# A hybrid diffusion layer with experts: the branch test, the gate and the last scatter at the end of the kernel

## The chip, the cores and the metric

The kernel runs on one core of one Trainium2 chip. The metric is the time of one launch on the device, in microseconds (us). TensorE (PE in the rows, PEld for its weight loads) multiplies matrices, VectorE (DVE), ScalarE (ACT) and GpSimd (POOL) work elementwise, and SyncE (SP) issues DMA transfers. A row with a q behind the engine's name (PEldq, ACTq) is an instruction that the engine's sequencer handles by itself, such as a branch.

## The reference, cut to what matters

128 context tokens and 128 latent tokens of width 1024 go through one layer. All 256 tokens share the weights, but each of the two groups has its own modulation vectors. The change touches only the end of this:

```python
# channel mixer: top 4 of 32 experts, combine holds the weight of each expert for each token
def expert(acc, xs):
    wu, bu, wd, bd, g = xs
    ...
    y = ((up + 1.0) * glu) @ wd + bd
    return acc + g[:, None] * y, None

xp = xp + gt_f * moe(h, *moe_args)      # gt_f: one vector of 1024 for the whole group
...
xs = xs + gt_f * moe(h, *moe_args)
y_prompt = rmsnorm(xp, g_final)         # x / sqrt(mean(x*x) + eps) * g_final
y_sample = rmsnorm(xs, g_final)
```

All matrices are float32. The 32 experts' weights are 384 MB of the 460 MB that the kernel reads.

## The kernel before, in words

The kernel is written engine by engine: each engine has its own instruction stream, and the order between them is made by semaphores alone (`wait_ge`, `then_inc`). No planner moves anything.

After the mixing part comes the loop over experts. It takes them in pairs, 16 pairs, two pairs to one turn of the loop (`Fori(0, PAIRS // BODY)`, 8 turns). One pair is a pass:

- TensorE gathers up to 64 tokens for each of the two experts with one-hot matmuls (`gather`, L1335), multiplies them by the up weights (L1372), transposes, and multiplies by the down weights (L1410). The last result stands in PSUM banks 6 and 7 (`YB`).
- ScalarE copies it to `yb` (L654), 128 slots by 1024, and raises `y_ready`.
- TensorE scatters the slots back to their tokens with the weights of the router: `scatter`, L1342, four matmuls of 128x512 into banks 4 to 7 (`GB + n`), for token group t = n // 2 and column half n % 2. The scatter of a pass is done in the middle of the next pass, so the scatter of the last pass is left over for the end. VectorE adds the four banks into `acc` (L975).
- SyncE streams the weights through a ring of 16 slots of 1 MB (L329), each load waiting until its slot is free (`moe_free`).

An expert has 64 places. If more tokens than that chose one expert, further rounds of all 16 passes are needed. Each engine has the code for up to three further rounds behind its loop, nested in `If`s (`further_rounds`, the test is L280), and steps over it when the count doesn't ask for it. In the runs here no further round is taken: each matmul group of the loop appears 16 times.

At the end, with the loop and the test behind:

- VectorE multiplies `acc` by the gate `gtf` and adds it to x (L1045, L1046), without the last pass. Then `last_add(t)` takes the last scatter: for each half a multiplication by the gate (L1052), a wait for it to finish (`link`), and an addition to x (L1053).
- ScalarE squares each half of x and sums it (`squares`, L603). VectorE adds the two sums of a token group (`mean_of_halves`, L699) and GpSimd raises that to the power -1/2 (`root`, L392).
- VectorE multiplies x by the final gain (`last_gain`, L1060, two halves). The scale by the root is shared: ScalarE does the low half (L674, `fin_lo`), VectorE the high half (`last_scale`, L1065, `fin_hi`).
- SyncE stores each group when both halves are done (L342), and waits for both stores.

Of the kernel before, what the change touches and what calls it, by code (L numbers as in the profile page):

```python
# [1 line left out]

# [7 lines left out]
ALU = mybir.AluOpType  # L23
ACT = mybir.ActivationFunctionType
# [3 lines left out]
D = 1024  # L28
# [11 lines left out]
HALF = 512  # L40
# [39 lines left out]
def layer_kernel(nc, A_x_prompt, A_x_sample, A_cache_k, A_cache_v, A_c, A_c_ctx, A_w_ada, A_b_ada, A_g_mix,  # L80
# [12 lines left out]
    with ExitStack() as ctx:  # L93
# [36 lines left out]
        def in_slot(s, at, *shape):  # L130
# [6 lines left out]
            if len(shape) == 3:  # L137
# [12 lines left out]
        hid = region(8960, D)  # L150
        hT = region(9984, KB, P)
        yb = region(11008, D)

        sgA = region(0, KB, TOK)
        sgB = region(2048, KB, TOK)
# [97 lines left out]
        cur_ready, glu_ready = sem("cur_ready"), sem("glu_ready")  # L253
        fin_ss, fin_lo, fin_hi, last_scat, stored = (sem("fin_ss"), sem("fin_lo"), sem("fin_hi"), sem("last_scat"),
                                                     sem("stored"))
        xf_ready = sem("xf_ready")
        kv_stored, bias_t, bias_copied = sem("kv_stored"), sem("bias_t"), sem("bias_copied")

        GB, YB = 4, 6
# [211 lines left out]
        def _(act):  # L471
# [150 lines left out]
            nc.scalar.activation(woT[0:E, :, :], ps[0:E, 6, 0:TOK].rearrange("p (a b) -> p a b", a=2),  # L622
                                 ACT.Copy).then_inc(woT_ready, 1)
            act.wait_ge(L["bdn"], 16)
            act.sem_inc(y_ready, 1)

            def xg_out(b, H, q):

# [4 lines left out]
            def body(I, r):  # L633
                P0 = act.snap(I * BODY)
                n0 = act.snap(I * BC)
                H0 = act.snap(P0 * 2 + (r + 1))
                for h in range(BODY):
                    Pn, H = P0 + h, H0 + 2 * h
                    xg_out(1, H, h)
                    for b in range(2):  # L640
                        act.wait_ge(g_ready, Pn * 2 + (b + 1))
                        nc.scalar.activation(sig[:, b * HALF:(b + 1) * HALF], gate[:, b * HALF:(b + 1) * HALF],  # L642
                                             ACT.Sigmoid, scale=ALPHA).then_inc(sig_ready, 1)
                    xg_out(0, H + 1, (h + 1) % 2)
                    act.wait_ge(woT_done, Pn + 2)
                    nc.scalar.activation(woT, ps[:, YB, 0:TOK].rearrange("p (a b) -> p a b", a=2),
                                         ACT.Copy).then_inc(woT_ready, 1)
                    for b in range(2):
                        act.wait_ge(hT_done, Pn * 2 + (b + 1))
                        nc.scalar.activation(hT[:, 4 * b:4 * b + 4, :],  # L650
                                             ps[:, GB + b, :].rearrange("p (a b) -> p a b", a=4),
                                             ACT.Copy).then_inc(hTe_ready, 1)
                    act.wait_ge(moe_free, n0 + (RING + (h + 1) * PC))
                    nc.scalar.activation(yb.rearrange("p (a b) -> p a b", a=2), ps[:, YB:YB + 2, :],  # L654
                                         ACT.Copy).then_inc(y_ready, 1)

            xg_out(0, 0, 0)
            more = read_flags(act)
# [20 lines left out]
        def _(dve):  # L679
# [352 lines left out]
            def run(r):  # L1032

                dve.wait_ge(oh_ready, r * (PAIRS + 1))
                V.tensor_scalar(tab[:, :, 0:4], tab[:, :, 0:4], float(CAP), None, ALU.subtract).then_inc(tab_ready, 1)
                dve.wait_ge(tab_ready, r)
                dve.wait_ge(gath_done, r * (2 * PAIRS + 1))
                one_hots(0, r * (PAIRS + 1))
                with dve.Fori(0, PAIRS // BODY) as i:
                    body(i + r * (PAIRS // BODY), i, r)  # L1040
                dve.wait_ge(acc_done, 4 * (r + 1) * PAIRS)
            further_rounds(dve, more, run)


            link(V.tensor_tensor(acc, acc, gtf[:, :, :], ALU.mult))  # L1045
            link(V.tensor_tensor(x[:, :, :], x[:, :, :], acc, ALU.add))  # L1046

            def last_add(t):
                for n in range(2):
                    c = slice(n * HALF, (n + 1) * HALF)  # L1050
                    dve.wait_ge(last_scat, 2 * t + n + 1)
                    link(V.tensor_tensor(acc[:, t, c], ps[:, GB + 2 * t + n, :], gtf[:, t, c], ALU.mult))  # L1052
                    V.tensor_tensor(x[:, t, c], x[:, t, c], acc[:, t, c], ALU.add).then_inc(fin_ss, 1)  # L1053

            def last_gain(t):

# [8 lines left out]
                V.tensor_scalar(x[:, t, HALF:D], x[:, t, HALF:D], rstd[:, t:t + 1], None, ALU.mult).then_inc(fin_hi, 1)  # L1065

            dve.wait_ge(L["gfin"], 16)
            last_add(0)
            last_add(1)
            mean_of_halves(0, 1)  # L1070
            last_gain(0)
            last_scale(0)
            mean_of_halves(1, 1)
            last_gain(1)
            last_scale(1)


        @block.tensor
        def _(pe):
# [256 lines left out]
                                 oh[:, t, :], start=(t == 0), stop=(t == 1))  # L1336
                ins.then_inc(gath_done, 1)

            def scatter(done):
                for n in range(4):  # L1340
                    t = n // 2
                    mm(ps[:, GB + n, :], woT[:, t, :], yb[:, (n % 2) * HALF:(n % 2 + 1) * HALF],  # L1342
                       start=True, stop=True).then_inc(done, 1)

            def body(I, r):
                P0 = pe.snap(I * BODY)
# [8 lines left out]
                for h in range(BODY):  # L1355
                    Pn, G, H = P0 + h, G0 + h, H0 + 2 * h

                    pe.wait_ge(u_read, Pn + 1)
                    pe.wait_ge(sel_ready, Pn + 1)
                    for n in range(4):  # L1360
                        for a in range(2):
                            mm(ps[CAP * a:CAP * a + CAP, n, :], selbuf[:, a, :], bparts[:, n * HALF:(n + 1) * HALF],
                               start=True, stop=False)
                    for kk in range(KB):
                        if kk % 4 == 0:
                            pe.wait_ge(xg_ready, H + (kk // 4 + 1))
                        if kk == 3:
                            gather(G - 1, 1)
                        w = [chunk(h * PC + 2 * kk + a) for a in range(2)]
                        for n in range(4):  # L1370
                            for a in range(2):
                                ins = mm(ps[CAP * a:CAP * a + CAP, n, :], xgT[:, h, kk, CAP * a:CAP * a + CAP],  # L1372
                                         w[a][:, n * HALF:(n + 1) * HALF], start=False, stop=(kk == KB - 1))
                                if n == 3:
                                    ins.then_inc(moe_free, 1)

                    pe.wait_ge(y_ready, Pn + 1)
                    pe.wait_ge(woT_ready, Pn + 1)
                    scatter(scat_done)

                    pe.wait_ge(acc_done, Pn * 4 + 1)
                    gather(G, 0)

                    pe.wait_ge(wo_ready, Pn + 1)
                    pe.wait_ge(acc_done, Pn * 4 + 3)
                    for t in range(2):
                        ins = tp(ps[:, YB, t * P:(t + 1) * P], wo[:, t, :], ident[:, :])  # L1387
                    ins.then_inc(woT_done, 1)

                    for f in range(KB):  # L1390
                        if f % 4 == 0:
                            pe.wait_ge(hid_ready, Pn * 2 + (f // 4 + 1))
                            if f == 0:
                                pe.wait_ge(xg_ready, H + 3)
                            else:
                                pe.wait_ge(acc_done, Pn * 4 + 2)
                        ins = tp(ps[:, GB + f // 4, (f % 4) * P:(f % 4 + 1) * P], hid[:, f * P:(f + 1) * P], ident[:, :])
                        if f % 4 == 3:
                            ins.then_inc(hT_done, 1)

                    pe.wait_ge(woT_ready, Pn + 2)
                    pe.wait_ge(acc_done, Pn * 4 + 4)
                    for f in range(KB):
                        if f % 4 == 0:
                            pe.wait_ge(hTe_ready, Pn * 2 + (f // 4 + 1))
                        if f % 2 == 0:
                            w = [chunk(h * PC + UPC + f + a) for a in range(2)]
                        for n in range(2):
                            for a in range(2):
                                ins = mm(ps[CAP * a:CAP * a + CAP, YB + n, :], hT[:, f, CAP * a:CAP * a + CAP],  # L1410
                                         w[a][:, (f % 2) * D + n * HALF:(f % 2) * D + (n + 1) * HALF],
                                         start=(f == 0), stop=(f == KB - 1))
                                if f % 2 and n == 1:
                                    ins.then_inc(moe_free, 1)
# [3 lines left out]
            more = read_flags(pe)  # L1418
            with pe.Fori(0, PAIRS // BODY) as i:
                body(i, 0)  # L1420
            pe.wait_ge(y_ready, 1 + PAIRS)
            pe.wait_ge(woT_ready, 1 + PAIRS)

            def run(r):
                gather(r * (PAIRS + 1), 0)
                with pe.Fori(0, PAIRS // BODY) as i:
                    body(i + r * (PAIRS // BODY), r)
                pe.wait_ge(y_ready, 1 + (r + 1) * PAIRS)
                pe.wait_ge(woT_ready, 1 + (r + 1) * PAIRS)
            further_rounds(pe, more, run)  # L1430
            scatter(last_scat)


_INS = ['x_prompt', 'x_sample', 'cache_k', 'cache_v', 'c', 'c_ctx', 'w_ada', 'b_ada', 'g_mix', 'w_in', 'w_pool',
# [24 lines left out]
```

## Time and profile before

| | |
|---|---|
| time, median of 3 runs | 1213.35 us (1212.09 to 1216.87) |
| span of the profiled execution | 1214.1 us |
| time given for the profiled execution beside its span | none |
| PE busy | 1066.4 us (88%) |
| DVE busy | 271.5 us (22%) |
| ACT busy | 161.5 us (13%) |
| mean granted TensorE clock | 0.984 of full speed |
| moved by DMA | 460.24 MB, mean 379 GB/s |
| end of the last matmul of the expert loop | 1194.6 us |
| from there to the end of the span | 19.5 us |

A start is counted from the first instruction of the profiled execution. "Idle before" is the time for which the engine had no busy instruction ahead of the one shown, and the arrow names what released it; "issue" means that the profile shows nothing that it waited for. A float32 matmul of 128x512 shows as two records.

### The profile page before, as it was taken

The page shows a single profiled execution, that of the slowest core. Times are in us where ns is not written, and L with a number is a line of the kernel's source. Part 1 is how long each engine was busy: PE and PEld are TensorE (multiplying, and loading weights), DVE is VectorE, ACT ScalarE, POOL GpSimd, SP SyncE. Part 2 cuts the span into 40 slices and gives each one's busy share as a digit, 9 for nine tenths or more (in the row PEclk, how much of TensorE's full clock was granted, in tenths as well). Part 3 has the DMA queues.
Part 4 walks back from the last instruction along what each step waited for, and adds up shares of the span by engine and source line. Part 5 has one row for each costly group of instructions (what it writes and reads, how often), then busy time and mean ns, then how long its engine had stood idle before and what let it go on. Part 6 is the DMA issues. An engine that isn't in the chain of part 4 may idle for free.

```text
span 1214.1 us, 14268 instructions
## 1 busy us (share of the span) xinstructions
PE 1066.4 (88%) x5363; PEld 523.7 (43%) x5363; DVE 271.5 (22%) x580; ACT 161.5 (13%) x275; POOL 54.6 (4%) x81
## 2 busy tenths in 40 slices
PE   4799999999999989797979797979798989898985
PEld 1574987554443434343434343433333333333331
DVE  2132856422021120202020202020202020202024
ACT  1101433211011101101110111011101110111011
POOL 3027000000000000000000000000000000000000
PEclk8899999989999999999999999999999999999998
DMA  9998553979999999999999999999999999999991
GB/s 356 363 345 314 211 202 112 368 308 419 415 419 416 420 415 420 415 421 415 421 415 420 415 421 414 421 414 421 414 422 414 421 414 421 414 421 413 422 412 59
DMA packets 88085, 460.24 MB, mean 379 GB/s; under 512 B 7404, under 2 KB 7448, under 8 KB 52120
## 3 DMA queue, kind: packets, MB, share of 16 engines
q1 hardware_dynamic: 86392, 455.12, 92.5%
q0 software_dynamic: 1024, 3.29, 1.0%
q10 hardware_dynamic: 640, 1.44, 0.4%
q8 instruction: 17, 0.28, 0.1%
q14 instruction: 12, 0.10, 0.0%
HBM read 458.26 MB, written 1.57 MB: 379 GB/s over the span
## 4 chain that ended last, share of the span: by engine, by line
SPq 57%; PE 26%; DMA 6%; issue 6%; DVE 4%; ACT 1%; POOL 0%; POOLq 0%; DVEq 0%; ACTq 0%
SPq L329 55%; PE ps L1372 7%; PE ps L1410 5%; DMA ring<-in_w_in_dram 4%; PE ps L1120 2%; PE ps L1303 2%; DMA ring<-in_w_up_dram 2%; PE ps L1117 1%; PE ps L1135 1%; PE ps L1137 1%; PE ps L1136 1%; SPq L321 1%; PE ps L1095 1%; PE ps L1335 1%; PE ps L1266 1%
## 5 line engine op out<-in xcount | busy, mean ns | idle before, releaser
L1372 PE MATMUL ps<-ring,arena 128*64 128x512 f32 x2048 | 460.8, 595 | 73.7 <-DMA ring<-in_w_up_dram 73.7
L1372 PEld LDWEIGHTS ps<-ring,arena 128*64 128x64 f32 x2048 | 160.0, 136 | 352.9 <-issue 349.2
L1410 PE MATMUL ps<-ring,arena 128*64 128x512 f32 x1024 | 224.9, 597 | 6.7 <-ACT arena L650 6.7
L1410 PEld LDWEIGHTS ps<-ring,arena 128*64 128x64 f32 x1024 | 86.6, 138 | 134.7 <-issue 134.7
L964 DVE COPY cur<-tab 128x8 f32 (+1 forms) x17 | 2.9, 171 | 448.9 <-PE ps L1335 448.8
L1000 DVE TENSOR_SCALAR arena<-ps 128x512 f32<-128x512 f32 x32 | 20.6, 686 | 329.6 <-PE ps L1372 329.6
L1335 PEld LDWEIGHTS ps<-arena 128*128 128x128 f32 x528 | 64.1, 195 | 21.5 <-issue 19.2
L1342 PE MATMUL ps<-arena 128*128 128x512 f32 x136 | 64.5, 618 | 5.0 <-issue 5.0
L1335 PE MATMUL ps<-arena 128*128 128x128 f32 x528 | 67.4, 282 | 0.4 <-DVE arena L968 0.4
L642 ACT ACTIVATE arena<-arena 128x512 f32<-128x512 f32 x32 | 19.6, 630 | 338.3 <-DVE arena L1000 338.3
L630 ACT ACTIVATE arena<-ps 128x512 f32<-128x512 f32 x33 | 19.7, 597 | 260.3 <-PE ps L1335 260.3
L1120 PE MATMUL ps<-ring 128*128 128x256 f32 x192 | 44.0, 392 | 6.0 <-issue 6.0
L654 ACT ACTIVATE arena<-ps 128x1024 f32<-128x1024 f32 x16 | 16.4, 1024 | 221.4 <-PE ps L1410 221.4
L1342 PEld LDWEIGHTS ps<-arena 128*128 128x128 f32 x136 | 25.1, 194 | 44.2 <-issue 44.2
L455 POOL COPY selbuf<-sel 96x128 bf16 x16 | 4.7, 291 | 867.7 <-DVE arena L1002 854.7
L1120 PEld LDWEIGHTS ps<-ring 128*128 128x128 f32 x192 | 37.8, 198 | 12.2 <-issue 6.8
L975 DVE TENSOR_TENSOR arena<-ps,arena 128x512 f32<-128x512 f32 x64 | 40.9, 680 | 0.0
L1135 PE MATMUL ps<-parts 128*128 128x256 f32 x128 | 36.7, 287 | 0.6 <-DVE parts L801 0.6
L1095 PE MATMUL ps<-ring 128*32 128x512 f32 x192 | 27.1, 689 | 10.5 <-DMA ring<-in_w_ada_dram 10.5
L1136 PE MATMUL ps<-parts 128*128 128x256 f32 x128 | 36.2, 283 | 0.0
L1137 PE MATMUL ps<-parts 128*128 128x256 f32 x128 | 36.2, 283 | 0.0
L1387 PE MATMUL ps<-ident,arena 128*128 128x128 f32 x32 | 7.0, 301 | 24.9 <-DVE arena L975 24.9
(212 smaller groups left out, 746.9 us busy)
## 6 DMA issues: line engine op xcount, KB each, us to landing
ring<-in_w_up_dram SPq DMA_DIRECT2D x256, 1024.0 KB, 24.1
ring<-in_w_down_dram SPq DMA_DIRECT2D x128, 1024.0 KB, 20.5
ring<-in_w_ada_dram SPq DMA_DIRECT2D x24, 1024.0 KB, 13.9
ring<-in_w_in_dram SPq DMA_DIRECT2D x16, 1024.0 KB, 12.5
ring<-in_w_out_dram SPq DMA_DIRECT2D x4, 1024.0 KB, 6.7
ring<-in_w_pa_dram SPq DMA_DIRECT2D x2, 1024.0 KB, 7.3
ring<-in_w_pb_dram SPq DMA_DIRECT2D x2, 1024.0 KB, 6.6
out_dram<-x SPq DMA_DIRECT2D x2, 512.0 KB, 2.6
```

The lines of the kernel that those rows point to most:

```text
L329: sp.dma_start(dst, src).then_inc(moe_loaded[n % RING], 16)
L975: V.tensor_tensor(acc[:, t, c], ps[:, GB + n, :], acc[:, t, c], ALU.add).then_inc(acc_done, 1)
L1095: ins = mm(ps[32 * q:32 * q + 32, bank, :], cs[:, kk, :], w[:, q * HALF:(q + 1) * HALF], start=(kk == 0), stop=(kk == KB - 1))
L1120: ins = mm(ps[:, bank + b // 2, (b % 2) * TOK:(b % 2 + 1) * TOK], wk[:, b * P:(b + 1) * P], hTm[:, kk, :], start=(kk == 0), stop=(kk == KB ...
L1135: mm(out, w_top[:, n % 2, kk, :], hT_top[:, kk, :], start=(kk == 0), stop=False)
L1136: mm(out, w_top[:, n % 2, kk, :], hT_rest[:, kk, :], start=False, stop=False)
L1137: ins = mm(out, w_rest[:, n % 2, kk, :], hT_top[:, kk, :], start=False, stop=(kk == KB - 1))
L1303: ins = mm(ps[:, 2 * t + n, :], sgA[:, kk, t * P:(t + 1) * P], wo_[kk // 2][:, kk % 2, n * HALF:(n + 1) * HALF], start=(kk == 0), stop=(kk ...
L1335: ins = mm(ps[:, GB + b, (j % 4) * P:(j % 4 + 1) * P], h2[:, t, j * P:(j + 1) * P], oh[:, t, :], start=(t == 0), stop=(t == 1))
L1342: mm(ps[:, GB + n, :], woT[:, t, :], yb[:, (n % 2) * HALF:(n % 2 + 1) * HALF], start=True, stop=True).then_inc(done, 1)
L1372: ins = mm(ps[CAP * a:CAP * a + CAP, n, :], xgT[:, h, kk, CAP * a:CAP * a + CAP], w[a][:, n * HALF:(n + 1) * HALF], start=False, stop=(kk ...
L1410: ins = mm(ps[CAP * a:CAP * a + CAP, YB + n, :], hT[:, f, CAP * a:CAP * a + CAP], w[a][:, (f % 2) * D + n * HALF:(f % 2) * D + (n + 1) * H ...
```

## The change

Four edits, all at the end, and one small one in each pass:

1. TensorE no longer waits for the last `yb` ahead of the test for further rounds. The test comes directly behind the loop, and the waits come after it. The same wait goes into the code of the further rounds for TensorE and VectorE.
2. The copy of `yb` out of PSUM (L654) is made in two halves of 128x512, in every pass, and each half raises `y_ready`. All counts of `y_ready` are doubled.
3. The last scatter is written on its own. VectorE first multiplies `yb` by the gate of each group into a new buffer `yg` (`last_weight`, four products of 128x512; `yg` lies over `gate` and `sig`, which are free by then). TensorE scatters `yg` into banks 0 to 3 instead of 4 to 7. Behind each scatter VectorE has one addition of PSUM to x in place of a multiplication and an addition.
4. VectorE takes the mean of the second group ahead of the high-half scale of the first: the order mean, gain, scale, mean, gain, scale becomes mean, gain, mean, gain, scale, scale.

```diff
+        yg = region(6912, 2, D)
...
-            act.sem_inc(y_ready, 1)
+            act.sem_inc(y_ready, 2)
...
-                    nc.scalar.activation(yb.rearrange("p (a b) -> p a b", a=2), ps[:, YB:YB + 2, :],
-                                         ACT.Copy).then_inc(y_ready, 1)
+                    for b in range(2):
+                        nc.scalar.activation(yb[:, b * HALF:(b + 1) * HALF], ps[:, YB + b, :],
+                                             ACT.Copy).then_inc(y_ready, 1)
...
+            def last_weight(t):
+                for n in range(2):
+                    c = slice(n * HALF, (n + 1) * HALF)
+                    dve.wait_ge(y_ready, 2 * PAIRS + n + 1)
+                    V.tensor_tensor(yg[:, t, c], yb[:, c], gtf[:, t, c], ALU.mult).then_inc(yg_ready, 1)
 
             def last_add(t):
                 for n in range(2):
                     c = slice(n * HALF, (n + 1) * HALF)
                     dve.wait_ge(last_scat, 2 * t + n + 1)
-                    link(V.tensor_tensor(acc[:, t, c], ps[:, GB + 2 * t + n, :], gtf[:, t, c], ALU.mult))
-                    V.tensor_tensor(x[:, t, c], x[:, t, c], acc[:, t, c], ALU.add).then_inc(fin_ss, 1)
+                    V.tensor_tensor(x[:, t, c], x[:, t, c], ps[:, 2 * t + n, :], ALU.add).then_inc(fin_ss, 1)
...
             dve.wait_ge(L["gfin"], 16)
+            last_weight(0)
+            last_weight(1)
             last_add(0)
             last_add(1)
             mean_of_halves(0, 1)
             last_gain(0)
-            last_scale(0)
             mean_of_halves(1, 1)
             last_gain(1)
+            last_scale(0)
             last_scale(1)
...
-                    pe.wait_ge(y_ready, Pn + 1)
+                    pe.wait_ge(y_ready, Pn * 2 + 2)
                     pe.wait_ge(woT_ready, Pn + 1)
-                    scatter(scat_done)
+                    scatter()
...
             with pe.Fori(0, PAIRS // BODY) as i:
                 body(i, 0)
-            pe.wait_ge(y_ready, 1 + PAIRS)
-            pe.wait_ge(woT_ready, 1 + PAIRS)
...
             further_rounds(pe, more, run)
-            scatter(last_scat)
+            pe.wait_ge(woT_ready, 1 + PAIRS)
+            for n in range(4):
+                t, c = n // 2, slice((n % 2) * HALF, (n % 2 + 1) * HALF)
+                pe.wait_ge(yg_ready, n + 1)
+                mm(ps[:, n, :], woT[:, t, :], yg[:, t, c], start=True, stop=True).then_inc(last_scat, 1)
```

## Rows read from the trace of the kernel before

**Rows 1.** Page, busy share of the DMA engines in 40 slices, in tenths.

```profile
DMA  9998553979999999999999999999999999999991
```

**Rows 2.** PE timeline, last passes: start, us, instructions, idle before.

```profile
1072.15 1.06 PE L1362 MATMUL ps<-bparts,selbuf 96*64 96x512 bf16 x8
...
1101.44 3.65 PE L1372 MATMUL ps<-ring,arena 128*64 128x512 f32 x16 [1.31 <-DMA ring<-in_w_up_dram]
...
1110.02 3.70 PE L1342 MATMUL ps<-arena 128*128 128x512 f32 x8
...
1178.92 15.64 PE L1410 MATMUL ps<-ring,arena 128*64 128x512 f32 x64 [0.30 <-ACT arena L650]
```

**Rows 3.** Chain that ended last, around the last copy of yb.

```profile
1194.61 1.03 ACT arena L654
1195.64 3.95 issue
1199.60 2.09 PE ps L1342 x2
```

**Rows 4.** Instructions of the test for further rounds, L280: min/median/max ns.

```profile
L280 ACTq COMPARE_BRANCH  x1: 50/50/50, 1194.7 to 1194.7; - x1
L280 PEldq COMPARE_BRANCH  x1: 3867/3867/3867, 1195.7 to 1195.7; - x1
```

**Rows 5.** TensorE's branch at the end of a loop turn, L1419.

```profile
L1419 PEldq COMPARE_BRANCH  x8: 76/208/265, 356.6 to 1190.2; - x8
```

**Rows 6.** Timeline from 1183 us on, all engines.

```profile
1183.59 2.29 DVE L1045 TENSOR_TENSOR arena<-arena,gtf 128x2048 f32<-128x2048 f32 x1 [5.74 <-issue]
1185.92 2.29 DVE L1046 TENSOR_TENSOR x<-x,arena 128x2048 f32<-128x2048 f32 x1
...
1201.81 0.69 DVE L1052 TENSOR_TENSOR arena<-ps,gtf 128x512 f32<-128x512 f32 x1 [13.59 <-PE ps L1342]
...
1206.58 0.69 DVE L1053 TENSOR_TENSOR x<-x,arena 128x512 f32<-128x512 f32 x1
1207.19 0.20 DVE L699 TENSOR_SCALAR small<-small 128x1 f32<-128x1 f32 x1
1207.31 0.63 ACT L603 ACTIVATE arena<-x 128x512 f32<-128x512 f32 x1 [0.60 <-DVE x L1053]
1207.32 1.28 DVE L1060 TENSOR_TENSOR x<-x,arena 128x512 f32<-128x512 f32 x2
...
1208.63 0.49 DVE L1065 TENSOR_SCALAR x<-x,small 128x512 f32<-128x512 f32 x1
1209.03 0.21 DVE L699 TENSOR_SCALAR small<-small 128x1 f32<-128x1 f32 x1
...
1209.25 2.19 SPq L342 DMA_DIRECT2D out_dram<-x  x2
1209.32 0.93 POOL L392 TENSOR_TENSOR small<-small,mhalf 128x1 f32<-128x1 f32 x1 [0.92 <-DVE small L699]
1210.34 0.72 ACT L674 ACTIVATE x<-x,small 128x512 f32<-128x512 f32 x1 [1.12 <-POOL small L392]
1210.47 0.49 DVE L1065 TENSOR_SCALAR x<-x,small 128x512 f32<-128x512 f32 x1
```

**Rows 7.** ACT timeline in the loop.

```profile
1057.70 1.09 ACT L650 ACTIVATE arena<-ps 128x512 f32<-128x512 f32 x2
...
1087.23 0.60 ACT L630 ACTIVATE arena<-ps 128x512 f32<-128x512 f32 x1 [12.51 <-PE ps L1335]
```

**Rows 8.** Windows: busy us (x instructions), then granted clock, DMA share, GB/s.

```profile
1175.50:1178.90 3.40, 1.57 (x13) 1.15 (x12) 2.32 (x4) 1.66 (x4) 0.00 (x0) 1.00 1.03 410
1178.90:1182.30 3.40, 3.38 (x8) 1.14 (x10) 0.00 (x0) 0.41 (x1) 0.00 (x0) 0.50 1.04 410
...
1199.40:1202.80 3.40, 3.20 (x4) 1.51 (x5) 0.96 (x2) 0.00 (x0) 0.00 (x0) 0.50 0.03 5
```

**Rows 9.** DMA from 1209 us on: GB/s in 40 slices of 0.1275 us.

```profile
GB/s 0 0 0 0 0 0 0 0 193 289 482 418 386 450 321 482 386 418 289 0 0 0 0 450 418 386 482 289 482 386 418 482 289 33 0 0 0 0 0 0
```

More of the change, by code:

```diff
@@ L255, in layer_kernel @@
                                                      sem("stored"))
-        xf_ready = sem("xf_ready")
+        xf_ready, yg_ready = sem("xf_ready"), sem("yg_ready")
         kv_stored, bias_t, bias_copied = sem("kv_stored"), sem("bias_t"), sem("bias_copied")
@@ L1041, in run @@
                 dve.wait_ge(acc_done, 4 * (r + 1) * PAIRS)
+                dve.wait_ge(y_ready, 2 * (1 + (r + 1) * PAIRS))
             further_rounds(dve, more, run)
@@ L1337, in gather, with scatter @@
                 ins.then_inc(gath_done, 1)
-            def scatter(done):
+            def scatter():
                 for n in range(4):
@@ L1342, in scatter @@
                     mm(ps[:, GB + n, :], woT[:, t, :], yb[:, (n % 2) * HALF:(n % 2 + 1) * HALF],
-                       start=True, stop=True).then_inc(done, 1)
+                       start=True, stop=True).then_inc(scat_done, 1)
             def body(I, r):
@@ L1427, in run @@
                     body(i + r * (PAIRS // BODY), r)
-                pe.wait_ge(y_ready, 1 + (r + 1) * PAIRS)
+                pe.wait_ge(y_ready, 2 * (1 + (r + 1) * PAIRS))
                 pe.wait_ge(woT_ready, 1 + (r + 1) * PAIRS)
             further_rounds(pe, more, run)
-            scatter(last_scat)
+            pe.wait_ge(woT_ready, 1 + PAIRS)
[3 more added lines that the diff above has]
+                mm(ps[:, n, :], woT[:, t, :], yg[:, t, c], start=True, stop=True).then_inc(last_scat, 1)
 _INS = ['x_prompt', 'x_sample', 'cache_k', 'cache_v', 'c', 'c_ctx', 'w_ada', 'b_ada', 'g_mix', 'w_in', 'w_pool',
```

## The prediction

> **What bounds the kernel now.** I read the page first. The DMA engines are busy at nine tenths from the tenth slice to the last but one [rows 1]: in the expert loop the weights set the pace. The timeline of TensorE says the same from inside: between groups of up matmuls it idles some 1.3 us for the next weights [rows 2]. Nothing in the change touches that stream, so a small cost inside a pass has room to hide. Only the last 19.5 us, from the last down matmul at 1194.56 (1178.92 + 15.64) [rows 2] to the end at 1214.1, have no transfer of weights beside them. There each step is paid in full, and there the edits lie. I therefore read the chain of waits from 1194 us on [rows 3], then the timeline of the tail [rows 6], then the branch instructions [rows 4, 5], and last the clock and the DMA in short windows [rows 8, 9].
>
> In the chain, ScalarE copies the last yb until 1195.64. Then come 3.95 us of "issue", and only then the scatter [rows 3]. The rows of the test say what this is: TensorE's branch at L280 begins at 1195.7, when the wait for yb ends, and takes 3867 ns [rows 4]. After it VectorE is the bound: its first product of gate and scatter starts at 1201.81, and its last addition at 1206.58 [rows 6]. I call the start of this last addition A. From A to the end are 7.5 us.
>
> **The test.** TensorE's sequencer runs ahead of its matmuls. It takes the branch at the end of the last turn at 1190.2, 4.4 us before the last matmul ends [rows 5, 2]. Today it then stops at the wait for yb. With the wait moved behind the test, the test begins at about 1190.3 and is done by 1194.2, under the last down matmuls. The work that hides it is that of rows 2. Nothing else is queued behind it but the scatter. If the cover were gone and the test began only at 1194.56, the scatter could start at 1198.5 and no sooner; that is the upper bound, 2.4 us more than I take below. The lower bound is zero.
>
> The row says 3.87 us for a test of which another engine's, ScalarE's, shows 50 ns [rows 4]. The Trainium skill, "Advanced Engine Details and Errata", section Control Flow Timing, gives about 108 ns for a compare-and-branch; by that figure, an estimate, moving the test would be worth 0.1 us and the whole sum would be about -2.1 us. The trace disagrees by its 3867 ns. "Runtime: NRT & Kernel Launch", section Instruction fetch mechanics, of the same skill, says that a taken branch to code that isn't loaded waits for a fetch of it, and with this the trace agrees.
>
> **The gate ahead of the scatter.** ScalarE starts the copy at 1194.61 [rows 3]. One copy of 128x512 takes 0.60 us and two take 1.09 [rows 7], so the halves are there at 1195.21 and 1195.70. VectorE begins 0.12 us after what it waits for (scatter done at 1199.60 + 2.09 = 1201.69, product at 1201.81 [rows 3, 6]). A product of this shape takes 0.69 us and two take 1.28 [rows 6], so one begins each 0.60 us. The four products end at 1196.02, 1196.6, 1197.2 and 1197.8. VectorE is free for them, as it finished its two long operations at 1188.2 [rows 6].
>
> The scatter starts at 1196.1 (0.1 us after the first product), not 1199.60: **-3.5 us**. At full clock the four matmuls take 3.70 us [rows 2], about 0.87 each, which is slower than the products arrive; so the last is done at 1199.8. VectorE adds the first three meanwhile (it can from 1197.8 on, one each 0.6 us) and starts the last addition at 1199.9. So A moves from 1206.58 to 1199.9. From the scatter's start to A it was 6.98 us and becomes 3.8: **-3.2 us**. Half of the elementwise work has left this chain (four of eight operations), and so has the first matmul's slow clock.
>
> The clock of the scatter is my first unknown. Before, TensorE idled 5 us and the granted clock in 1199.40:1202.80 was 0.50 [rows 8], which is the 1.2 GHz level. The new idle time is 1.5 us. Idle times of 1.3 us recur in the loop at full clock [rows 2]; but once, after 3.40 us with only 1.57 us of TensorE work, the clock stood at 0.50 for the next 3.40 [rows 8]. The bounds are 0 and 1.7 us, half of such a stretch. I take 0, as the new gap has 15.64 us of unbroken work ahead of it [rows 2]. "TensorE: Matmul & The Clock Gate", section What's actually happening, of the Trainium skill, says that throttled is the default and activity releases it; by that a gap speaks for the slow level, and the sum would be -4.2 us.
>
> The banks 0 to 3 cost nothing: they hold the up products, which VectorE has read before the down matmuls can begin. The split copy costs 0.07 us in each pass (1.09 against 1.02). ScalarE has 12.5 us of idle time behind it [rows 7], and the scatter that waits for yb comes at 1110.02, 38 us after the pass's beginning at 1072.15 [rows 2]. I take 0; bare, it would be 16 x 0.07 = 1.1 us.
>
> **Means first.** Now from A on. The mean of the second group sat behind the first group's scale, which waited for GpSimd: mean at 1209.03, which is A + 2.45 [rows 6]. It needs the fourth square, which starts at A + 0.73, lasts 0.63 and a short read-out, so about A + 1.5. In the new order it follows the first gain, which ends at 1207.32 + 1.28 = 1208.60, A + 2.0. The second gain then runs to A + 3.4 (0.13 + 1.28 after the mean). GpSimd's root reaches ScalarE 1.31 us after the mean (1209.03 to 1210.34): A + 3.3, and ScalarE's half is done at A + 4.0. VectorE's two scales of 0.49 us stand now one behind the other: done at A + 3.85 and about A + 4.25. Before they ended at 1209.12 and 1210.96, A + 2.5 and A + 4.4.
>
> So the second group gains 0.1 us, and the first loses 1.3. What is late next is the first store, and it meets the second. SyncE issues 0.13 us after the scale. Each store has its data under way 0.87 us after issue and moves it for 1.4 us at around 400 GB/s, and the two never overlapped [rows 9]. Now the first moves from A + 4.85 to A + 6.25 and the second behind it to about A + 7.6, where it ended at 1213.33, A + 6.75, before. That costs **+0.8 us**; bounds 0 (they overlap freely) and 1.4 (one whole transfer).
>
> **Sum.** -3.5 - 3.2 + 0.8 = -5.9 us, against this execution's own span: 1214.1 to 1208.2. No other time is given for that execution; its span lies 0.8 us above the median of the runs, 1213.35. Taken off the median, 1207.4 us, which is 0.49% less.
>
> **Rivals.**
> 1. *The test stays on the path.* If the sequencer doesn't come as far ahead as in rows 5, the scatter starts at 1198.5, 2.4 us later: 1209.8. The branch at 1190.2 speaks against it. Chance 0.05.
> 2. *The scatter runs at the slow clock*: +1.7 us, 1209.1. Rows 8 show both cases. Chance 0.10.
> 3. *ScalarE becomes the bound.* Its own test is at 1194.7 [rows 4], and nothing shows how soon it can go on, since today it is wanted only after the first addition, behind 1201.81 [rows 6]. VectorE's first instruction behind its test came after 5.74 us of idle time [rows 6], under full DMA traffic; TensorE's took 3.87 in a quiet stretch. ScalarE's first square is wanted at 1198.4. By 3.87 it is ready at 1198.6 and the lag is made up; by 5.74 at 1200.4, its second square ends at 1201.9 where the mean wanted it at 1200.5, and all behind comes 1.5 us later: 1208.9. Its stretch is a quiet one, so the first is nearer. Chance 0.10.
> 4. *Slower than before.* The changed streams are laid out anew. If a turn of TensorE's loop no longer stayed loaded, each of 7 branches back would cost 3.87 us in place of 0.208 [rows 5], 26 us if bare: 1233. TensorE idles four or five times 1.3 us per pass [rows 2], over 10 us a turn, which would cover all of it; the branch would have to cost some 12 us each to decide. No turn before shows it. Chance 0.02.
> 5. *The stores don't meet* or share the engines better: 1206.6. Chance 0.13.
>
> **How the numbers follow.** The forecast itself has 0.60: 1207.4, its own range 1206.4 to 1208.4. The three runs before spread over 4.8 us, from 1.3 below the median to 3.5 above, so the median of the new kernel carries some 1 to 2 us of its own. The range reaches from rival 5 less 1.3 us, 1205.3, to rivals 2 and 3 together (1.7 + 1.5 above the forecast) with 1 us more, 1211.6. About 0.5% is what a measurement of this kernel can tell from no change, and the limit, 1207.3 us, lies at the forecast. Faster by over 0.5%: nearly half of the forecast's 0.60, all of rival 5, and strays of the rest, 0.44. Within 0.5%: 0.54. Slower: 0.02.
>
> **What the profile after would show.** TensorE's test at L280's successor begins near 1190.3, before the last down matmul ends, and the scatter follows the first gate product by 0.1 us. The clock across the scatter is 1.0. Four products and four additions stand on VectorE, the last addition starting about 5.4 us after the last down matmul. The squares follow their additions without a gap (rival 3: the first one waits on "issue"). The two stores are issued 0.4 us apart and their data runs for 2.7 us in one piece. What would make the prediction wrong is a scatter that starts later than 2 us after the last matmul, a first square later than 4.1 us after it, or stores that take more or less than 2.7 us together.

## The result, and the profile after

| | before | changed |
|---|---|---|
| median | 1213.98 us (1212.09 to 1216.87, 4 runs) | 1206.70 us (1204.28 to 1208.45, 4 runs) |
| span of the profiled execution | 1214.1 us | 1204.5 us |
| tail: last down matmul's end to the span's end | 19.6 us | 13.5 us |

The ratio is 0.994, with a 95% interval of 0.9921 to 0.9959: faster by 0.6%. I had forecast 1207.4 us, 0.49% less. Timed a second time (e9 below), the changed kernel came to 0.9951 (0.9937 to 0.9966), which is 0.49% less. So the gain lies on the 0.5% that the prediction took as the limit of what can be told from no change.

"Tail" stands for the time from the end of the last down matmul to the end of the span, here and below. For the kernel before it is 19.57 us; the table of before has 19.5 because it subtracts rounded times.

The tail is where the edits are, and it can be read far more finely than the runs. This is the timeline of the changed kernel from 1183 us on (start, length, instructions, idle before). Rows are left out at the dots, and the weight loads everywhere. The first PE row is only the part of the last down matmuls that falls into this window:

```profile
1181.55 2.29 DVE L1035 TENSOR_TENSOR arena<-arena,gtf 128x2048 f32<-128x2048 f32 x1 [5.63 <-issue]
1182.59 8.35 PE L1407 MATMUL ps<-ring,arena 128*64 128x512 f32 x38
...
1190.98 1.09 ACT L643 ACTIVATE arena<-ps 128x512 f32<-128x512 f32 x2 [13.61 <-PE ps L1407]
1191.71 2.50 DVE L1042 TENSOR_TENSOR arena<-arena,gtf 128x512 f32<-128x512 f32 x4 [5.54 <-ACT arena L643]
1192.55 3.67 PE L1430 MATMUL ps<-arena 128*128 128x512 f32 x8 [1.61 <-DVE arena L1042]
1194.13 1.96 DVE L1048 TENSOR_TENSOR x<-x,ps 128x512 f32<-128x512 f32 x3
1194.84 0.63 ACT L591 ACTIVATE arena<-x 128x512 f32<-128x512 f32 x1 [2.77 <-DVE x L1048]
...
1196.26 0.69 DVE L1048 TENSOR_TENSOR x<-x,ps 128x512 f32<-128x512 f32 x1 [0.17 <-PE ps L1430]
...
1198.19 0.20 DVE L688 TENSOR_SCALAR small<-small 128x1 f32<-128x1 f32 x1
1198.31 1.28 DVE L1055 TENSOR_TENSOR x<-x,arena 128x512 f32<-128x512 f32 x2
...
1199.51 0.87 DVE L1060 TENSOR_SCALAR x<-x,small 128x512 f32<-128x512 f32 x2
1200.09 0.85 SPq L330 DMA_DIRECT2D out_dram<-x  x2
```

The last down matmul ends at 1182.59 + 8.35 = 1190.94. The scatter starts 1.6 us later, where it was 5.0 [rows 2 and 3 for before], and what ends TensorE's idle time is now the gate's product and no longer "issue". The last addition starts 5.3 us after the last down matmul, where it was 12.0 [rows 2 and 6]. From there to the end it is 8.2 us, where it was 7.5: that part has grown.

The branches of the changed kernel, L1416 at the end of a loop turn and L268 for the test, answer to [rows 4, 5]:

```profile
L1416 PEldq COMPARE_BRANCH  x8: 76/208/256, 356.3 to 1186.6; - x8
```

```profile
L268 PEldq COMPARE_BRANCH  x1: 3726/3726/3726, 1186.7 to 1186.7; - x1
L268 ACTq COMPARE_BRANCH  x1: 50/50/50, 1191.2 to 1191.2; - x1
```

The test still takes TensorE 3.7 us. It starts 4.2 us before the last down matmul ends, so it is over 0.5 us before that end.

What takes TensorE so long at this branch was not tested: no run leaves the code of the further rounds out. The traces do show that instructions are fetched just then. Queue q8 is an instruction queue. It moves nothing between 360 us and the test in the kernel before, and in the test it moves one packet of 16 KB, in the kernel before (1195.6 to 1199.6 us) as in the changed one (1186.6 to 1190.5 us). The rows give packets, MB, and the share of 16 engines:

```profile
q8 instruction: 1, 0.02, 2.2%
```

```profile
q8 instruction: 1, 0.02, 2.1%
```

Granted clock and DMA (compare [rows 8, 9]):

```profile
1190.90:1192.50 1.60, 0.04 (x2) 0.00 (x0) 0.79 (x2) 1.09 (x2) 0.00 (x0) 1.00 0.05 10
1192.50:1196.30 3.80, 3.67 (x8) 1.44 (x8) 3.63 (x7) 1.46 (x5) 0.00 (x0) 1.00 0.00 0
```

```profile
DMA  0000000000000069979989989999989996000000
GB/s 0 0 0 0 0 0 0 0 0 0 0 0 0 0 273 425 425 303 455 394 364 485 425 334 425 394 425 425 425 334 425 394 394 243 0 0 0 0 0 0
```

The clock column (ahead of the last two) is 1.00 through the 1.6 us of waiting and the whole scatter. The second fence is the DMA from 1199 to 1204.4 us, in 40 slices of 0.135 us, first the busy share of the engines in tenths and then GB/s: the two stores move their data in one piece of 20 slices, 2.7 us, with no gap in it, where [rows 9] have two pieces with a gap.

### The profile page after: what moved, and what is told of

Read it like the earlier page. It is cut to its first block, busy times and chain, and to the rows that moved or that the text cites. A ratio compares the mean times of both kernels' runs of the same rounds, so it can differ in the third digit from the quotient of the medians.

```text
span 1204.5 us, 14284 instructions
## 1 busy us (share of the span) xinstructions
PE 1065.4 (88%) x5363; PEld 520.2 (43%) x5363; DVE 270.7 (22%) x580; ACT 162.3 (13%) x291; POOL 54.4 (5%) x81
## 4 chain that ended last, share of the span: by engine, by line
SPq 49%; PE 29%; DMA 10%; issue 5%; DVE 5%; ACT 1%; DVEq 0%; POOL 0%; ACTq 0%
SPq L317 47%; PE ps L1369 8%; DMA ring<-in_w_up_dram 7%; PE ps L1407 7%; PE ps L1117 2%; PE ps L1300 2%; DMA ring<-in_w_ada_dram 2%; DMA ring<-in_w_in_dram 2%; PE ps L1114 1%; PE ps L1132 1%; PE ps L1134 1%; PE ps L1092 1%; PE ps L1133 1%; PE ps L1332 1%; SPq L309 1%
## 5 line engine op out<-in xcount | busy, mean ns | idle before, releaser
L630 ACT ACTIVATE arena<-arena 128x512 f32<-128x512 f32 x32 | 19.6, 630 | 336.4 <-DVE arena L989 336.4
L1339 PE MATMUL ps<-arena 128*128 128x512 f32 x128 | 59.2, 605 | 0.0
L618 ACT ACTIVATE arena<-ps 128x512 f32<-128x512 f32 x33 | 19.7, 597 | 257.0 <-PE ps L1332 257.0
L643 ACT ACTIVATE arena<-ps 128x512 f32<-128x512 f32 x32 | 17.4, 595 | 224.7 <-PE ps L1407 224.7
```

## The experiments

I measure each by its tail, since that repeats: the changed kernel's is 13.5 us in both of its profiles. Whole runs scatter by more than most edits are worth.

### e1: the kernel before with the test first, alone

```diff
-            pe.wait_ge(y_ready, 1 + PAIRS)
-            pe.wait_ge(woT_ready, 1 + PAIRS)
...
             further_rounds(pe, more, run)
+            pe.wait_ge(y_ready, 1 + PAIRS)
+            pe.wait_ge(woT_ready, 1 + PAIRS)
             scatter(last_scat)
```

> The kernel before with edit 1 alone: TensorE waits for the last yb behind the test, all else as it was. The tail, from the end of the last down matmul to the end of the span, was 19.6 us before and is 13.5 us in the changed kernel. Theory (the test hides under the last down matmuls): the scatter starts 1.2 us after the last down matmul in place of 5.0, at full clock, so its first result comes in 1.1 us and not 2.1; behind it stays VectorE's chain of eight operations. Tail 14.8 us. Rival (the test was not what cost, the waiting for yb was): the scatter stays at 5 us, tail 19.6.

Measured: tail 14.7 us; 1209.04 us median (7 runs) against 1213.54 (17 runs), ratio 0.995 (0.9934 to 0.9965). From its timeline and chain of waits:

```profile
1194.01 1.02 ACT L654 ACTIVATE arena<-ps 128x1024 f32<-128x1024 f32 x1 [15.31 <-PE ps L1410]
1195.08 3.70 PE L1342 MATMUL ps<-arena 128*128 128x512 f32 x8 [1.12 <-ACT arena L654]
```

```profile
1195.04 0.04 issue
1195.08 1.14 PE ps L1342 x2
```

The 3.95 us of issue have become 0.04, and the first result of the scatter comes in 1.14 us where it took 2.09 [rows 3]. The edit is worth 4.9 of the 6.0 us: the scatter starts 3.9 us sooner after the last down matmul, and its first result takes 0.95 us less.

### e2: the changed kernel without the test first

```diff
             with pe.Fori(0, PAIRS // BODY) as i:
                 body(i, 0)
+            pe.wait_ge(y_ready, 2 * (1 + PAIRS))
```

> The changed kernel with edit 1 undone: TensorE waits for both halves of yb ahead of the test. Theory: the scatter starts 5.0 us after the last down matmul in place of 1.6, and at the slow clock for some 3 us of it; the last addition starts at 10.4 in place of 5.3, tail 18.6 us. If the clock stays full, 17.0 us. Rival (edit 3 gives most of the gain by itself): tail under 15 us.

Measured: tail 18.4 us; 1213.17 us median (10 runs) against 1213.54 (17 runs), ratio 1.0 (0.9988 to 1.0011).

```profile
1192.37 2.50 DVE L1042 TENSOR_TENSOR arena<-arena,gtf 128x512 f32<-128x512 f32 x4 [5.50 <-ACT arena L643]
1196.46 5.31 PE L1431 MATMUL ps<-arena 128*128 128x512 f32 x8 [4.86 <-issue]
```

```profile
1191.60:1196.40 4.80, 0.00 (x0) 0.00 (x0) 2.50 (x4) 1.09 (x2) 0.00 (x0) 0.99 0.01 3
1196.40:1199.70 3.30, 3.24 (x4) 1.51 (x5) 0.69 (x1) 0.44 (x1) 0.00 (x0) 0.50 0.02 5
```

The gate's products are ready 1.6 us before TensorE can use them (1192.37 + 2.50 against 1196.46). The clock is at 0.50 as soon as the scatter starts. So the gate's edit needs the test's: edits 2 to 4 without edit 1 shorten the tail by 1.1 us, and the whole time can't tell that from nothing.

### e3 and e11: the old order of the scales

```diff
             last_gain(0)
+            last_scale(0)
             mean_of_halves(1, 1)
             last_gain(1)
-            last_scale(0)
             last_scale(1)
```

> The changed kernel with edit 4 undone: gain, scale, mean, gain, scale. Theory (means first costs, as it makes the stores meet): the time from the last addition's start to the end of the span goes back from 8.2 us to 7.5, tail 12.9 us. Rival (the earlier mean pays): tail 13.5 us or more.

> The changed kernel with the old order of the scales again. Tail 12.9 us, 0.65 us less than the changed kernel; median by as much under it if nothing else differs.

Measured: tail 12.9 us both times, 0.7 less than the changed kernel. Medians 1206.57 us (4 runs; the ones before 1213.54) and 1207.61 (6 runs; before 1212.87), ratios 0.994 (0.992 to 0.996) and 0.9948 (0.9932 to 0.9965).

```profile
1197.22 2.19 SPq L330 DMA_DIRECT2D out_dram<-x  x2
...
1198.44 0.49 DVE L1060 TENSOR_SCALAR x<-x,small 128x512 f32<-128x512 f32 x1
```

The first store is issued at 1197.22, 2.7 us after the last addition's start (1194.55) and not 3.8; the second scale ends 4.4 us after it, against 4.1 in the changed kernel. Edit 4 does what it says, and costs more than it brings.

### e4: the copy of yb in one piece

```diff
-                    for b in range(2):
-                        nc.scalar.activation(yb[:, b * HALF:(b + 1) * HALF], ps[:, YB + b, :],
-                                             ACT.Copy).then_inc(y_ready, 1)
+                    nc.scalar.activation(yb.rearrange("p (a b) -> p a b", a=2), ps[:, YB:YB + 2, :],
+                                         ACT.Copy).then_inc(y_ready, 2)
```

> The changed kernel with the copy of yb in one piece of 128x1024. Theory: the first product of the gate starts 0.43 us later (1.02 against 0.60 us), all behind moves with it, tail 13.9 us; nothing changes inside the loop. Rival (the split costs in each pass): the time falls by up to 1 us though the tail grows.

Measured: tail 14.0 us, 0.5 more; the scatter waits 2.10 us instead of 1.61. Median 1209.4 us (5 runs), ratio 0.9958 (0.9942 to 0.9974). The loop itself, from SyncE's branch at the end of its first turn to that of its last, takes 844.2 us here, with the copy in one piece, and 844.2 us in the changed kernel (325.4 to 1169.6, see e9):

```profile
L319 SPq COMPARE_BRANCH  x8: 40/45/50, 325.7 to 1169.9; - x8
```

So the split costs nothing that shows in the passes.

### e5: the gate behind the scatter

```diff
-            last_weight(0)
-            last_weight(1)
...
-                    V.tensor_tensor(x[:, t, c], x[:, t, c], ps[:, 2 * t + n, :], ALU.add).then_inc(fin_ss, 1)
+                    link(V.tensor_tensor(acc[:, t, c], ps[:, 2 * t + n, :], gtf[:, t, c], ALU.mult))
+                    V.tensor_tensor(x[:, t, c], x[:, t, c], acc[:, t, c], ALU.add).then_inc(fin_ss, 1)
...
-                pe.wait_ge(yg_ready, n + 1)
-                mm(ps[:, n, :], woT[:, t, :], yg[:, t, c], start=True, stop=True).then_inc(last_scat, 1)
+                pe.wait_ge(y_ready, 2 * PAIRS + n % 2 + 1)
+                mm(ps[:, n, :], woT[:, t, :], yb[:, c], start=True, stop=True).then_inc(last_scat, 1)
```

> The changed kernel with the gate behind the scatter again (product and addition for each bank, as before), but with halves of yb, banks 0 to 3 and the test first. Theory: the scatter starts at 0.7 us after the last down matmul in place of 1.6, but eight operations of VectorE follow its first result; the last addition starts at 6.7 us in place of 5.3. Tail 14.9 us against 13.5. Rival (the scatter's four matmuls are the bound either way): tail 13.0 us or less.

Measured: tail 15.0 us (one run, 1208.01 us).

```profile
1191.74 3.67 PE L1429 MATMUL ps<-arena 128*128 128x512 f32 x8 [0.79 <-ACT arena L643]
1192.98 0.69 DVE L1048 TENSOR_TENSOR arena<-ps,gtf 128x512 f32<-128x512 f32 x1 [6.72 <-PE ps L1429]
...
1197.68 0.69 DVE L1049 TENSOR_TENSOR x<-x,arena 128x512 f32<-128x512 f32 x1
```

The scatter starts earlier, 0.8 us after the last down matmul, and it is over at 1195.41. VectorE needs till 1197.68 to begin its last addition. With the gate ahead, TensorE's 3.67 us are the bound instead: 1.4 us less.

### e6: one store only

The store of y_prompt is left out, so that output is not written.

```diff
-                sp.dma_start(y[0], x[:, t, :]).then_inc(stored, 16)
-            sp.wait_ge(stored, 32)
+                if t == 1:
+                    sp.dma_start(y[0], x[:, t, :]).then_inc(stored, 16)
+            sp.wait_ge(stored, 16)
```

> The changed kernel without the store of y_prompt (left out of the computation: that output is not written), to see what the meeting of the two stores costs. Theory: the second store's data starts 0.87 us after its issue and lasts 1.4 us, the end comes 3.0 us after the issue, 7.3 us after the start of the last addition in place of 8.2; tail 12.6 us. Rival (the stores overlap freely): tail 13.5 us.

Measured: tail 12.6 us, 0.9 less (one run, 1207.02 us). The store is issued at 1201.86 and the span ends at 1204.9, 3.0 us later. In the changed kernel the second store is issued at 1200.6 and the span ends 3.9 us later. So the meeting of the stores costs 0.9 us by this run. In the changed kernel the DMA engines are busy to six to nine tenths in every slice of the 2.7 us, and the second store has to wait for them.

### e7 and e10: gain and scale of the high half in one operation

`last_gain` does the low half only in these.

```diff
+                V.scalar_tensor_tensor(out=x[:, t, HALF:D], in0=x[:, t, HALF:D], scalar=rstd[:, t:t + 1],
+                                       in1=gfin[:, HALF:D], op0=ALU.mult, op1=ALU.mult).then_inc(fin_hi, 1)
...
             last_gain(0)
             mean_of_halves(1, 1)
-            last_gain(1)
             last_scale(0)
+            last_gain(1)
             last_scale(1)
```

> The changed kernel with the high halves' gain and scale in one operation of VectorE, (x * root) * gain, in the order mean, gain of the low half, mean, fused, gain of the low half, fused. VectorE's work behind the last addition falls from 3.8 us to about 3.2. Theory: first store 1.3 us earlier, second 0.3 us earlier, they still touch; from the last addition's start to the end 7.1 us in place of 8.2, tail 12.4 us. Rival (the chain over GpSimd and ScalarE is the bound, not VectorE): tail 13.0 us or more.

> The kernel with fused gain and scale again. Tail 12.4 us. If only the tail differs, its median lies 1.15 us under that of the changed kernel, an amount that the spread of the runs can hide. Rival (the other layout of the code costs something ahead of the tail): its median is again over that of the changed kernel by 1 us.

Measured: tail 12.4 us both times, 1.15 less than the changed kernel. Medians 1207.86 us (5 runs; before 1212.17), ratio 0.9958 (0.9942 to 0.9974), and 1205.74 us (6 runs; before 1212.87), ratio 0.9946 (0.9929 to 0.9963).

```profile
1200.47 0.75 DVE L1057 SCALAR_TENSOR_TENSOR x<-x,small,arena 128x512 f32<-128x512 f32 x1 [0.16 <-POOL small L380]
...
1201.14 0.68 DVE L1053 TENSOR_TENSOR x<-x,arena 128x512 f32<-128x512 f32 x1
1201.33 1.64 SPq L330 DMA_DIRECT2D out_dram<-x  x2
```

The first store is issued 2.7 us after the last addition's start (1198.62), the second 4.0. This is the shortest tail I found. The second time its median was the lowest of the three kernels beside it, the first time it was over the changed kernel's. Its intervals and the changed kernel's overlap, so the fused kernel is better by its tail and not shown to be by its time.

### e8: when ScalarE can go on behind its test

```diff
+            nc.scalar.activation(misc[:, 14:15], mhalf[:, :], ACT.Copy)
             for t in range(2):
                 squares(t, fin_ss)
```

> The changed kernel with one tiny ScalarE operation (a 128x1 copy to a scratch column) directly behind ScalarE's test, which begins about 0.25 us after the last down matmul's end. It waits for nothing, so its start shows when ScalarE's code behind the test is there. My third rival put that at 3.87 to 5.6 us after the test. Theory now: the first square started 3.6 us after the test and was released by the addition, so the code is there sooner: 3.1 us if it has to be fetched as in the kernel before, 0.1 us if it is loaded already. Tail 13.5 us either way.

Measured (one run, 1206.8 us; tail 13.5 us): the test at 1191.6, and

```profile
1191.41 1.09 ACT L643 ACTIVATE arena<-ps 128x512 f32<-128x512 f32 x2 [13.61 <-PE ps L1408]
1192.38 0.20 ACT L658 ACTIVATE small<-mhalf 128x1 f32<-128x1 f32 x1
```

The probe follows the copies at once, 0.8 us after the test. ScalarE waited for no code in this layout. In the changed kernel itself the first square is released by its addition, and not by "issue" (its row is above). The first square was wanted 3.6 us after the test in the changed kernel.

### e9: the changed kernel again

> The changed kernel itself, beside the next two on the same chip. So far the tail of each profile came out as the theory wants within 0.2 us, while the medians of whole runs did not follow in the same order: the kernel with the fused gain has a tail 1.15 us shorter and a median 1.2 us longer. Theory: the stretch ahead of the tail, whose code is the same in all of them, varies by several us from run to run, so the end of the last down matmul moves and the tail does not. Expected: tail 13.5 us, a median of 1205.5 to 1208.5.

Measured: tail 13.5 us; 1207.18 us median (6 runs) against 1212.87 (11 runs), ratio 0.9951 (0.9937 to 0.9966). The part ahead of the tail can be followed by SyncE's branch at the end of each loop turn (L319). In e3, in the changed kernel and in e11, whose code for the loop is the same:

```profile
L319 SPq COMPARE_BRANCH  x8: 40/45/50, 323.7 to 1167.8; - x8
```

```profile
L319 SPq COMPARE_BRANCH  x8: 40/45/50, 325.4 to 1169.6; - x8
```

```profile
L319 SPq COMPARE_BRANCH  x8: 40/45/50, 328.9 to 1173.1; - x8
```

From the first turn's end to the last's it is 844.1 to 844.2 us in all three. The end of the first turn itself lies anywhere in 5.2 us. The kernel before has its branch at L331 and takes 844.1 us too:

```profile
L331 SPq COMPARE_BRANCH  x8: 40/45/50, 327.4 to 1171.5; - x8
```

In all 13 profiles the loop takes 843.5 to 844.3 us, and the end of the first turn lies between 323.7 and 328.9 us. So most of what scatters these executions is ahead of the loop's second turn. The loop and the tail repeat. Between them the last pass can add 1.7 us, when a stretch at clock 0.50 falls into its down matmuls (they then take 15.6 us in place of 13.95). That is so in the profiles of the kernel before and of e1, and in none of the other eleven. The changed kernel's profile has such stretches too, but inside the loop, as here:

```profile
634.98 15.65 PE L1407 MATMUL ps<-ring,arena 128*64 128x512 f32 x64 [0.54 <-ACT arena L638]
```

Whether the new code moves the stretch out of the last pass or chance does is not shown.

## Why the prediction was right

Measured tails put side by side, each worked out as a difference of two of them (before rounding):

| edit | comparison | us |
|---|---|---|
| 1, test first | before 19.6, e1 14.7 | -4.9 |
| 2, halves of yb | e4 14.0, changed 13.5 | -0.5 |
| 3, gate ahead of the scatter | e5 15.0, changed 13.5 | -1.4 |
| 2 and 3 together, banks included | e1 14.7, e3 12.9 | -1.8 |
| 4, means first | e3 12.9, changed 13.5 | +0.7 |
| all | before 19.6, changed 13.5 | -6.0 |

- **The test.** Forecast: begun 4.3 us before the last down matmul's end, hidden wholly, scatter 3.5 us earlier. Measured: begun 4.2 us before, scatter 3.4 us earlier. e1 and e2 show it from both sides. The test was over only 0.5 us before the last down matmul ended; in the eleven profiles of kernels with the test first it took 3.35 to 3.91 us, and in the longest of them (e9) only 0.3 us were left. The Trainium skill's 108 ns for a compare-and-branch ("Advanced Engine Details and Errata", Control Flow Timing) would have left e1 at 19.5 us, an estimate from that figure; e1 measured 14.7. The next 1.6 us, copy and product, are further cover.
- **From the scatter's start to the last addition.** Forecast -3.2, to 3.8 us; measured 3.7 us (1192.55 to 1196.26), -3.3. The bound became TensorE's four matmuls, as forecast.
- **The clock.** Full, as I took it. After 1.6 us of idle time it stood at 1.00, after 4.86 us (e2) at 0.50. That was not one lucky profile: the four matmuls took 3.67 to 3.70 us in all eleven profiles with the test first, and 5.29 and 5.31 us in the two without (before, e2). Part of what edit 1 brings is this: the first result of the scatter comes 0.95 us sooner (e1).
- **Means first.** Forecast +0.8, measured +0.7 (e3), with the reason: the first store 1.2 us later, the second 0.2 sooner, and both in one piece of 2.7 us (e6).
- **Rivals.** The test did not stay on the path, the scatter was not slow, ScalarE was not the bound (e8), the branch at the end of a turn kept its 208 ns (row L1416), and the stores did meet.

Two things were off beside the sum. I set the span of the profiled execution against the median, as if a time were a span. It isn't: in the 36 runs of the kernel before that stand beside the experiments the time is 1.68 to 1.78 us over its span, and so it is in e1's seven. By that, an estimate, the profiled execution before took 1215.8 us, and not 0.8 but some 2.5 us more than the median that I had. This did no harm, as only the -5.9 us were taken off the median.

The other is a term that I had at nothing without saying so: what the change does outside the span. In the four runs of the changed kernel the time is 2.05 to 2.13 us over the span, and it is 2.03 to 2.13 in all runs of e2 to e7 and e9 to e11 (e8's one run: 1.90). So the change costs some 0.35 us that no profile shows, and e1 doesn't pay it, so it comes with edits 2 to 4 or with the other layout of the code. Which, is open. With it the 6.0 us of the tail are worth 5.7 us of time.

The spans of the two profiles differ by 9.6 us: 6.0 are the tail, 1.7 the stretch at clock 0.50 in the last down matmuls of the kernel before [rows 8], and 2.0 came before the end of the loop's first turn (327.4 against 325.4), where profiles with the same code for the loop differ by more (e9). The medians differ by 7.3 us, with 5.0 to 9.6 inside the interval, and by 5.7 in e9; the 5.7 us explain both, and for the 1.6 us more in the first no cause is shown. That the first median came within 0.7 us of the forecast is in part luck. The medians of the other kernels fell by 2.5 us less (e7) to 0.6 us more (e3) than their tails and the 0.35 us say (the tail alone for e1).

## What to carry to other kernels

Look for "issue" in the chain behind a branch, and ask whether the sequencer could have taken that branch earlier: a test that depends on nothing late belongs ahead of the last wait, where the queued work covers it. An elementwise factor that commutes with a matmul can be applied ahead of it, but this pays only if the matmul isn't already held up by something else (e2). When two results leave at the end, delaying the first one to hasten the second can cost more than it brings, since they then queue for the same DMA engines. When a part of the program scatters by more than the edit is worth, compare the stretch around the edit, not the spans. And compare time with time: what a profile doesn't span can change too, here by 0.35 us.

## What the runs showed of the hardware

- A branch over the unused rounds took TensorE 3.35 to 3.91 us in all 13 profiles, and the others' sequencers 45 to 63 ns at the branch itself, though VectorE's first instruction behind it came 5.7 us later before and 5.5 us later in the changed kernel.
- One packet of 16 KB on instruction queue q8 falls into TensorE's test, before and changed; from 360 us to the test the kernel before has none on it.
- ScalarE's code behind its test was there within 0.8 us (e8), which I had not expected, since I took the two slower cases as its bounds.
- TensorE's sequencer took its last branch of the loop 4.4 us (before) and 4.3 us (changed) ahead of the end of the matmuls.
- Two stores of 512 KB took 1.4 us each when alone [rows 9] and 2.7 us together when issued 0.5 us apart: they gain nothing from each other.
- The time of a run was 1.68 to 1.78 us over its span for the kernel before and e1, and 2.03 to 2.13 us for the changed kernel and its variants but e8 (1.90).
